# A decoder layer on eight cores: attention groups 16-4-1 instead of 1-4-16, one values block per unit, normalisation by token block

## What is computed

```python
h = rms_norm(x, g_pre_mix); proj = h @ w_in          # q, k, v: 12 heads of 64, pool input u, two gates
q = apply_rope(q); k = apply_rope(k)
for gi, (window, dilation) in enumerate(((128, 1), (512, 4), (2048, 16))):   # 4 heads per group
    o_g, lse_g = dilated_window_attention(q[hs], k[hs], v[hs], window, dilation)
wts = softmax(stack(lses), axis=groups)
o_attn = sum(wts * outs)                              # groups combined by their denominators
y_pool = multiscale_pool(u, w_mix, scale)             # trailing means over 2, 4, 8, 16 tokens
merged = sigmoid(gate_a) * (o_attn @ w_proj_attn) + sigmoid(gate_p) * (y_pool @ w_proj_pool)
x = x + rms_norm(merged @ w_out, g_post_mix)
x = x + rms_norm((silu(a) * b) @ w_down, g_post_ffn)  # a, b = halves of rms_norm(x) @ w_gate_up
```

## Time and profile before

| | us |
|---|---|
| median of 3 runs | 1012.27 (1010.47 to 1012.73) |
| profiled execution, device time | 1016.44 |
| span of its slowest core (core 4), from its first to its last instruction | 1014.9 |
| spans of the 8 cores | 1001.8 to 1014.9 |
| attention on core 4, from the first values block to the first gate matmul | 220.9 to 335.1 |

### The profile page before, as it was taken

How to read it: one execution, slowest core, us unless ns; L and a number is a source line. 1 busy time by engine, 2 the same in 40 slices (tenths; PEclk the granted TensorE clock), 3 DMA queues, 4 the chain that set the end, 5 groups by cost and what they waited for, 6 DMA issues and landing times.

```text
span 1014.9 us, 15115 instructions; the slowest of 8 cores (1001.8 to 1014.9 us)
## 1 busy us (share of the span) xinstructions
PE 930.8 (92%) x5448; PEld 469.9 (46%) x5532; DVE 403.1 (40%) x554; ACT 341.2 (34%) x588; POOL 334.8 (33%) x324
## 2 busy tenths in 40 slices
PE   1569999999897999999998999999999999999993
PEld 1327554447674444444444444444444444444441
DVE  2566786548978522232577222121112122121111
ACT  3426663339776522223564111111101111111100
POOL 2462787663401353332566111111332000001231
PEclk9769999999999899999999999999999999999997
DMA  8988310000022171211978766764434544430432
GB/s 232 247 181 235 81 64 21 1 1 2 2 44 43 43 125 21 42 22 26 286 264 193 143 108 113 123 108 71 125 104 125 84 75 71 83 63 1 125 107 81
DMA packets 32586, 98.50 MB, mean 97 GB/s; under 512 B 4224, under 2 KB 4224, under 8 KB 32512
## 3 DMA queue, kind: packets, MB, share of 16 engines
q0 software_dynamic: 15296, 41.92, 24.9%
q1 hardware_dynamic: 17072, 55.58, 17.1%
q10 hardware_dynamic: 144, 0.03, 0.0%
HBM read 122.64 MB, written 16.78 MB: 137 GB/s over the span
## 4 chain that ended last, share of the span: by engine, by line
PE 81%; issue 4%; DVE 4%; DMA 3%; POOL 3%; ACT 2%; SPq 0%; DVEq 0%; POOLq 0%; ACTq 0%
PE ps L1185 15%; PE ps L1151 15%; PE ps L1154 15%; PE ps L438 12%; PE ps L925 6%; PE ps L928 5%; PE ps L518 5%; DMA xst<-xh 2%; DMA xin<-xo 2%; PE ps L420 2%; PE ps L935 1%; PE ps L932 1%; PE ps L482 1%; PE ps L792 1%; POOL x1b L1001 1%
## 5 line engine op out<-in xcount | busy, mean ns | idle before, releaser
L1151 PE MATMUL ps<-hT,wgu 128*128 128x512 bf16 x659 | 157.6, 379 | 0.7
L1154 PE MATMUL ps<-hT,wgu 128*128 128x512 bf16 x658 | 157.5, 379 | 0.7
L1185 PE MATMUL ps<-wdn,ffT 128*128 128x512 bf16 x690 | 151.5, 379 | 1.0 <-DMA wdn<-wdn 0.2
L1166 DVE TENSOR_TENSOR ffT<-ps,sa 128x512 bf16<-128x512 f32 x88 | 60.7, 690 | 222.6 <-PE ps L1154 222.6
L1165 ACT ACTIVATE sa<-ps 128x512 f32<-128x512 f32 x88 | 52.5, 597 | 241.4 <-PE ps L1151 241.4
L1185 PEld LDWEIGHTS ps<-wdn,ffT 128*128 128x128 bf16 x704 | 68.8, 98 | 83.5 <-issue 0.7
L1154 PEld LDWEIGHTS ps<-hT,wgu 128*128 128x128 bf16 x672 | 65.8, 98 | 79.3
L1151 PEld LDWEIGHTS ps<-hT,wgu 128*128 128x128 bf16 x672 | 65.6, 98 | 78.6
L74 POOL DMA_DIRECT2D wgu<-wgu x42 | 22.6, 537 | 236.2 <-PE ps L1154 227.5
L438 PE MATMUL ps<-hT,wqk 128*128 128x512 bf16 x374 | 89.4, 379 | 2.0 <-DVE uh L631 1.4
L1001 POOL TENSOR_TENSOR x1b<-tb,xin 128x1024 f32<-128x1024 f32 x31 | 72.9, 2350 | 55.0 <-DVE tb L996 27.9
(11 more groups left out here) (120 smaller groups left out, 1200.8 us busy)
## 6 DMA issues: line engine op xcount, KB each, us to landing
wgu<-wgu POOLq DMA_DIRECT2D x42, 512.0 KB, 5.2
xst<-xh SPq DMA_DIRECT2D x16, 512.0 KB, 19.1
xin<-xo SPq DMA_DIRECT2D x16, 512.0 KB, 6.0
x1s<-x1b SPq DMA_DIRECT2D x16, 512.0 KB, 4.3
xin<-x1s SPq DMA_DIRECT2D x16, 512.0 KB, 5.2
out<-x1b SPq DMA_DIRECT2D x15, 512.0 KB, 3.6
xst<-xo SPq DMA_DIRECT2D x12, 512.0 KB, 7.4
wdn<-wdn POOLq DMA_DIRECT2D x22, 256.0 KB, 6.1
```

Of the source, the lines that this page charges most:

```text
L1151: e1 = pe.op(lambda e, k=k, wbuf=wbuf, ba=ba, tok=tok: e.matmul(ps[:, ba, :], lhsT=wbuf[:, 0, k, :], rhs=hT[:, k, tok], start=(k == 0), st ...
L1154: e2 = pe.op(lambda e, k=k, wbuf=wbuf, bb=bb, tok=tok: e.matmul(ps[:, bb, :], lhsT=wbuf[:, 1, k, :], rhs=hT[:, k, tok], start=(k == 0), st ...
L1166: ef = dve.op(lambda e, ub=ub, bb=bb, j=j, b=b: e.tensor_tensor(out=ffT[:, j, b * 512:(b + 1) * 512], in0=ps[:, bb, :], in1=sa[ub][:, :], ...
L1185: ev = pe.op(lambda e, j=j, h2=h2, pr_=pr_, il=il: e.matmul(ps[:, pr_[0] + h2, :], lhsT=ffT[:, j, il * 128:(il + 1) * 128], rhs=wdn[:, j, ...
```

## The change

Four things are moved; no arithmetic is added or removed.

- The groups run 16, 4, 1. ACT's copy into `acc` is now that of dilation 16, and the last additions on DVE are those of dilation 1. The rope order of the last quarter, the places of `wvr`, of the values blocks and of two weight buffers follow. All three groups go through s_, half, pr in that order, so the last group finishes token block after token block.
- One values block per unit: `u + 4` are done by iteration u, the last in iteration 44.
- ACT waits for the end of rope only ahead of the exp of unit 2, DVE ahead of its first pooling step. DVE's pooling steps move one iteration back (1 to 8), the means of the POOL chains to 14, 15 and 21, 22, `pool_mix` to 12 to 15 and 25 to 28; the loads of the merge's first weights are issued in iteration 29 (before: 37).
- Normalisation takes both pairs of heads at once for a block of 512 tokens: Ln and Exp (1024 per row) in iterations 38, 42, 46 and behind the loop, the product on DVE in iterations 40, 44, 48 and behind the loop. POOL has no product any more.

```diff
     def load_wv(g):
-        wload("wv%d" % g, wvr[:, g, :, :], wv_d[g])
+        wload("wv%d" % g, wvr[:, 2 - g, :, :], wv_d[g])
...
-        order = (6, 10, 7, 11, 8, 9, 0, 4, 1, 5, 2, 3) if b < 3 else (6, 0, 7, 1, 10, 8, 11, 9, 4, 5, 2, 3)
+        order = (6, 10, 7, 11, 8, 9, 0, 4, 1, 5, 2, 3) if b < 3 else (10, 4, 11, 5, 8, 2, 9, 3, 6, 0, 7, 1)
...
-    act.wait(ev_qk, dve.last(), pool.last())
-    dve.wait(ev_qk, pool.last())
+    ev_rope = [ev_qk, dve.last(), pool.last()]
...
-        if g == 0:
+        if g == 2:
             ev2 = act.op(lambda e: e.activation(out=dst, in_=src, func=AF.Copy), waits=[ev])
...
-    units = [(g, s_, half, pr) for g in range(2) for s_ in range(4) for half in range(2) for pr in range(2)]
-    units += [(2, s_, half, pr) for pr in range(2) for s_ in range(4) for half in range(2)]
+    units = [(g, s_, half, pr) for g in (2, 1, 0) for s_ in range(4) for half in range(2) for pr in range(2)]
...
-    def att_norm(pr, b, eng):
+    def norm_inv(b):
         tok = slice(b * 512, (b + 1) * 512)
...
+        ev_ln = act.op(lambda e: e.activation(out=acc[:, 1, :, tok], in_=acc[:, 1, :, tok], func=AF.Ln), waits=[acc_ev[(0, b)], acc_ev[(1, b)]])
+        norm_ev[b] = act.op(lambda e: e.activation(out=acc[:, 1, :, tok], in_=acc[:, 1, :, tok], func=AF.Exp, scale=-1.0), waits=[ev_ln])
+
+    def norm_mul(b):
+        tok = slice(b * 512, (b + 1) * 512)
+        ev_oT[b] = dve.op(lambda e: e.tensor_tensor(out=oT2[:, :, tok], in0=acc[:, 0, :, tok], in1=acc[:, 1, :, tok], op=ALU.mult),
+                          waits=[norm_ev[b], acc_ev[(0, b)], acc_ev[(1, b)], ev_q2])
...
-    v_list = [(0, 0, 1 + n) for n in range(16)] + [(1, n // 4, 1 + n % 4) for n in range(16)] + [(2, n, 1) for n in range(16)]
+    v_list = [(2, n, 1) for n in range(16)] + [(1, n // 4, 1 + n % 4) for n in range(16)] + [(0, 0, 1 + n) for n in range(16)]
...
+        if u == 2:
+            act.wait(*ev_rope)
...
-        while nv < min(len(v_list), 6 * (u + 4) // 5):
+        while nv < min(len(v_list), u + 4):
...
-        if 0 <= u < 8:
-            c0_steps[u]()
-            if u == 7:
+        if 1 <= u < 9:
+            dve.wait(*ev_rope)
+            c0_steps[u - 1]()
+            if u == 8:
...
-        if 22 <= u < 26:
-            pool_mix(1, u - 22)
+        if 25 <= u < 29:
+            pool_mix(1, u - 25)
...
-        if u >= 41 and u % 2 == 1 and u < 48:
-            att_norm(0, (u - 41) // 2, pool)
-    for b in range(4):
-        att_norm(1, b, dve if b % 2 == 0 else pool)
+        if u >= 38 and u % 4 == 2 and u < 50:
+            norm_inv((u - 38) // 4)
+        if u >= 40 and u % 4 == 0:
+            norm_mul((u - 40) // 4)
+    norm_inv(3)
+    norm_mul(3)
```

More of the change, by code:

```diff
@@ L517, in v_block @@
         for k in range(8):
-            ev = pe.op(lambda e, k=k: e.matmul(ps[:, bank, 0:256], lhsT=tok_ap_fn(k), rhs=wv_tile[:, g, k, :], start=(k == 0), stop=(k == 7)),
+            ev = pe.op(lambda e, k=k: e.matmul(ps[:, bank, 0:256], lhsT=tok_ap_fn(k), rhs=wv_tile[:, 2 - g, k, :], start=(k == 0), stop=(k == 7)),
                        signal=(k == 7))
@@ L860, in build_program @@
                     f()
[L861 to L865 removed]
+        if 12 <= u < 16:
+            pool_mix(0, u - 12)
+        if u in (14, 15):
+            h10[1][u - 14]()
+            if u == 15:
                 for f in h11[0]:
                     f()
[L868 to L871 removed]
+        if u in (21, 22):
+            h11[1][u - 21]()
+        if 25 <= u < 29:
+            pool_mix(1, u - 25)
             ev_yp = act.last()
@@ L874, in build_program @@
             att_apply(napp)
+            if napp == 15:
+                ev_g2 = pe.last()
             napp += 1
-        if u == 37:
-            assert nv == len(v_list)
-            ev_v = pe.last()
+        if u == 29:
             wg_ev = [pool.dma(wgs[i][:, :, :, :], wg_d[i], d_wg[i], waits=[ev_wz[1]]) for i in range(2)]
-            pool.dma(wpa[:, :, :], wpa_d[:, :, :], d_wm2, waits=[ev_v])
+            pool.dma(wpa[:, :, :], wpa_d[:, :, :], d_wm2, waits=[ev_g2])
             ev_wp = pool.dma(wpp[:, :, :], wpp_d[:, :, :], d_wm2)
-        if u >= 41 and u % 2 == 1 and u < 48:
-            att_norm(0, (u - 41) // 2, pool)
-    for b in range(4):
-        att_norm(1, b, dve if b % 2 == 0 else pool)
+        if u >= 38 and u % 4 == 2 and u < 50:
[4 more added lines that the diff above has]
+    norm_mul(3)
+    assert nv == len(v_list) and len(ev_oT) == 4
     tap("hT", hT[:, :, :])
```

30 lines of the change are left out of this document (10 added, 20 removed).

## The result

| us | before | after |
|---|---|---|
| median (12 executions each, taken together) | 1012.14 | 1007.04 |
| lowest to highest | 1010.47 to 1013.92 | 1003.87 to 1010.07 |
| span of the profiled execution's slowest core | 1014.9 (core 4) | 1002.3 (core 5) |
| attention, first values block to first gate matmul: that core | 114.2 | 106.3 |
| the same, median of the 8 cores (lowest to highest) | 112.95 (111.7 to 114.2) | 106.4 (106.3 to 106.8) |

The ratio of after to before is 0.9938, with a 95% interval of 0.9925 to 0.9952: the change makes the kernel 0.62% faster, some 6.3 us. The two medians of the table differ by 5.1 us, which is still within that interval. The forecast was 10.7 us, so the direction is right, the time (1007.04) lies just inside the range (996.5 to 1007.5), and four tenths of the gain are missing.

A forecast was written before the change was run, and what follows sets the result against it. Attention was read as PE's stage, 93 us of work in 114.2. Start gains 3.3, middle about 0.8 worse, shorter tail: first gate at 324.4 instead of 335.14, so 1012.27 - 10.7 = 1001.6 us; range 996.5 to 1007.5.

The forecast's parts named there:

- The 0.55 us of the earlier trace: Middle of attention: a DVE mask ends 0.55 us after the POOL operation beside it, one mask per POOL operation.

The follow-up runs named there:

- experiment 2: Changed kernel with token block 2's Ln and Exp behind the exp of unit 47 and its product behind the loop; ratio 0.9901 to the kernel before.
- experiment 7: Changed kernel with block 2's Ln and Exp behind unit 47's exp, first `pool_mix` half in iterations 18 to 21, products of blocks 1 and 2 behind the loop; 997.45 us.
- experiment 5: Kernel before with only ACT's wait for rope moved to the exp of unit 2 and DVE's to its first pooling step; ratio 0.9949 to before.
- experiment 10: Changed kernel with ACT's and DVE's waits for all of rope put back ahead of the first values block; ratio 0.9922 to the kernel before.

## What to carry to other kernels

Account for a tail with the queues as late as the units before leave them, and put nothing between the last exps and masks that isn't needed until the next stage: normalisation moved out of the way gave 4.0 us of the stage here (2.45 in experiment 2, 1.55 in 7), more than half of what the change itself gave (6.55). Where two engines are each near the limit, the waits for one don't add to those for the other: the price of a slower operation is what remains when the other engine's waits shrink. And read the length of a stage from all cores before a sum is made against it: behind one and the same wait the clock may fall on some cores and not on others.

## What the runs showed of the hardware

**A strided fp32 write on ACT.** 128x512 fp32 from PSUM into every 16th fp32 of a row: 0.82 to 0.89 us from start to start, recorded 1.11 to 1.52. Contiguous: 0.47 to 0.50, recorded 0.59 to 0.70. The Trainium skill, "SBUF — State Buffer", section "Door 1: The DMA port swizzle", has SBUF lines of 16 bytes and a penalty for each access that goes to a new one; here a write that touches a new line with each element takes 1.7 to 1.9 times as long on ACT, in agreement.

**Masks beside POOL.** The 0.55 us of the earlier trace rows repeat: four masks from 243.06 on end 0.54 to 0.56 after the four operations of POOL's first chain (the last of each):

```profile
249.83 2.04 DVE L778 TENSOR_TENSOR PT<-PT,masks 128x1024 bf16<-128x1024 bf16 x1 [0.73 <-ACT PT L773]
```

```profile
248.70 2.62 POOL L703 TENSOR_TENSOR Z<-Y 64x1025 f32<-64x1025 f32 x1
```

The mask ends at 251.87, the POOL operation at 251.32. The Trainium skill, "SBUF — State Buffer", section "Who interferes with whom", says that a DVE instruction with two SBUF inputs contends with a GpSimd instruction that reads SBUF, and that the lock between them is exclusive. The masks' ends agree. Whether POOL waits in its turn these rows don't show: in this chain its operations are recorded 0.14 to 0.15 us behind each other, while the mask still runs.

**The clock.** Behind the wait for the mean, 2.72 and 2.70 us long, the granted clock was 0.62 on one core and 1.00 on another of the same execution (experiment 5), with 2.7 us of difference in the stage; in the kernel before it stayed at 1.00 behind 3.0 us on core 2. Behind waits of 1.00, 0.24, 1.37, 0.57 and 0.57 in experiment 2 the gate matmuls ran low on core 5 (3.40 for what takes 1.89) and at full clock on core 3. What decides between the cores these runs don't show. On all eight cores alike, the low clock followed the wait of 2.1 at the start of the kernel before (0.65 from 225 to 228 on core 4), and none followed the wait of 1.15 there in experiment 10, five waits of 0.28 to 1.05 us in the changed kernel (264 to 275 on core 5), or 1.00, 0.24, 0.24, 0.60 and 0.57 at the end of experiment 7.
